# Attention results in other PSUM banks, and four merge gate units inside the NSA loop

## The chip, the cores and the metric
One core of one Trainium2 chip runs the whole program. The metric is the device time of one execution in microseconds (us); of the kernel before it was taken three times, and the median is used. TensorE is called PE, VectorE DVE, ScalarE ACT, GpSimd POOL and SyncE SP, as in the profile.

## The reference, cut to what matters
Three layers over 512 tokens of width 1024, float32: an HGRN2 layer with a SwiGLU feed-forward, a dilated-window attention layer with another, and a layer that adds two mixers, NSA (block-sparse attention) and GLA, through learned merge gates. The two parts that the change touches:

```python
# layer 2: 12 heads, in 3 groups of 4 with windows of dilation 1, 4 and 16
q, k = apply_rope(u @ w_q), apply_rope(u @ w_k); v = u @ w_v
for group, heads in enumerate(...):            # softmax over its own window
    out_g, lse_g = dilated_window_group(q, k, v, window, dilation)
alpha = softmax(lse, over the three groups)    # weighs the groups
h = h + (o * alpha) @ w_out
# layer 3: merge of the two mixers
gate_a, gate_b = split(sigmoid(u @ w_merge))   # each 1024 wide
merged = gate_a * (o_nsa @ w_up_nsa) + gate_b * (o_gla @ w_up_gla)
x = x + merged @ w_out
```

## The kernel before, in words
Activations lie feature-major, [128 partitions, chunk, 512 tokens]. To keep float32 accuracy each projection is made of three products per chunk of 128 features: high weight by high activation, high by low, low by high. `unit(section, k, act, bank)` is one output tile of 128 features: 8 chunks of 3 products, into one PSUM bank (there are 8, `ps[:, bank]`); lines 412 to 414.

**Weights.** SP streams each unit's weights into a ring of 4 slots, each load behind `w_used` (units that PE has finished). ACT casts them to the high half (`hi`, L1102), POOL subtracts to get the low half (`lo`, L1583). There are two slots for split weights, so the cast of unit n+2 waits until PE has used unit n, and PE waits on `w_lo`. `ahead(section, k)` is that cast or subtraction for the unit two after k. The queues of ACT and POOL are in program order, so the place of each `hi` and `lo` in them matters.

**Attention.** V is made token-major, group by group, in four banks each: 0 to 3, 4 to 7, 0 to 3 (L626 to L628); ACT evicts them (L1329, semaphore `av_ready`, 4 for each group). Then 24 `qk_tile`s follow, six for each head step j. Tile N goes to bank N % 4; ACT copies it (`take_raw`, L1341), DVE multiplies by the sine (L2094), POOL by the cosine (L1684), DVE adds (L2101, `qk_ready`). Tile 0 waits until all of V is evicted, tiles from 4 on until DVE has read the bank's last tenant (`rope_sin`).
A head step j on PE is: three QK tiles of step j+1, `attn_scores(j)` (L675 to L683, into banks 4 to 7: group 0 in 4 and 5, group 1 in 6, group 2 in 7), three more QK tiles (in step 3 four tiles of the output projection), and `attn_core(j)`. There PE transposes the probabilities back into the same banks (L706), for groups 1, 2 and 0; ACT copies each to SBUF (L1374, L1374, L1372 for the two banks of group 0; `pt_ready`), and PE multiplies by V (L715 for groups 1 and 2, L718 and L721 for group 0) into bank 4 + g. All values wait for all three copies, since group 1's bank 5 and group 2's bank 6 still hold transposes of others. ACT takes the results (L1379, `ao_hi`), DVE the rest (`ao_rest`, L2154, `ao_lo`), and `attn_out` (L696 to L698) multiplies them with w_out: units 0 to 3 and 8 to 11 take heads 0 and 1, units 4 to 7 and 12 to 15 heads 2 and 3. Unit 4 waits for all twelve results.
On DVE a step is: two ropes, `masked_max` for three groups, a rope, `mix_tops`, `weigh`, two ropes, `ao_rest`, a rope.

**NSA loop.** 24 steps, six for each of four pairs of heads, (query tile, branches) in the order 3a, 3b, 0ab, 2a, 2b, 1ab. In step e PE makes `nsa_scores(e + 2)` (L1005), `nsa_transposes(e)` (L1017), `nsa_values(e - 1)` (L1033) and `gate_chunks(e)`. DVE scales the probabilities (`nsa_scale`, L2425), ahead of each step's transposes, masks and reduces the scores, and adds a pair's values once per pair (`nsa_add`, L2435); ACT takes exponentials (L1521) and copies transposes (L1529). `gate_chunks` puts 1 to 3 chunks of a merge gate unit (a `unit("merge", k)`, 8 chunks, bank 7) behind the values of a step, as `GATE_AT` says: {step: (unit, first chunk, last + 1)}. When a unit is complete, DVE reads it (`merge_raw`, L2441), and the next unit waits for that.
**Merge loop.** For each of 8 output tiles j: gate units (j, 0) and (j, 1) unless made in the NSA loop, then one up-projection unit (L1083 to L1085), sigmoids on ACT (L1561), products and sum on DVE (L2469, L2470, L2475). The host lays out the merge weights in the order of use, which `merge_at(j, k)` mirrors.

Of the kernel before, what the change touches and what calls it, by code (L numbers as in the profile page):

```python
# [4 lines left out]
F32 = mybir.dt.float32  # L5
# [6 lines left out]
P = 128  # L12
# [81 lines left out]
def program(nc, a, out):  # L94
# [20 lines left out]
    with ExitStack() as ctx:  # L115
# [45 lines left out]
        def views(used=0):  # L161
            at = [used]

            def take(*shape):
# [8 lines left out]
                if len(shape) == 3:  # L173
# [79 lines left out]
        prob = shared[:, 0:3072].rearrange("p (a h n) -> p a h n", a=3, h=2)  # L253
        probT = shared[:, 3072:5120].rearrange("p (a h n) -> p a h n", a=2, h=2)

        GATES = ((0, 0), (0, 1), (1, 0))
        GATE_AT = {0: (0, 0, 3), 1: (0, 3, 4), 2: (0, 4, 6), 3: (0, 6, 7), 4: (0, 7, 8),
                   7: (1, 0, 1), 8: (1, 1, 3), 9: (1, 3, 4), 10: (1, 4, 5), 11: (1, 5, 7), 12: (1, 7, 8),
                   15: (2, 0, 1), 16: (2, 1, 2), 17: (2, 2, 4), 18: (2, 4, 5), 19: (2, 5, 6), 20: (2, 6, 8)}
        GATE_END = {4: 0, 12: 1, 20: 2}  # L260

        def merge_at(j, k):

            return {(1, 0): 2, (0, 2): 3}.get((j, k), 3 * j + k)

        TILE_STEPS = ((3, (0,)), (3, (1,)), (0, (0, 1)), (2, (0,)), (2, (1,)), (1, (0, 1)))
        PER_PAIR = len(TILE_STEPS)
# [23 lines left out]
        take = views(used=2 * HC * T)  # L291
        msig, mtmp = take(4, T), take(2, T)
        assert 2 * HC * T + 6 * T <= 28 * T

        def tokens(g, b):

# [95 lines left out]
        def _(pe):  # L392
# [265 lines left out]
                    used(m)  # L658

            def qk_tile(N):  # L660
                if N >= 4:
                    pe.wait_ge(s["rope_sin"], 2 * (N - 3))
                elif N == 0:
                    pe.wait_ge(s["av_ready"], GROUPS * TT)
                used(unit("attn_qk", N, us, N % 4))

            def attn_scores(j):
                pe.wait_ge(s["qk_ready"], 6 * (j + 1))
# [18 lines left out]
            def attn_out(k):  # L687

                n, second = k // 8 * 4 + k % 4, k % 8 // 4
                rr, v, _ = split_use("attn_out", k)  # L690
                pe.wait_ge(s["w_lo"], v)
                rows = ps[:, n].rearrange("p (b m) -> p b m", b=TT)
                for c in range(6):
                    g, j, w = c % 3, 2 * second + c // 3, slice(c * P, (c + 1) * P)
                    oh, ol = ao_split[:, 0, g * HPG + j], ao_low(g, j)
                    nc.tensor.matmul(ps[:, n], ws[:, 0, rr, w], oh, start=not second and c == 0, stop=False)  # L696
                    nc.tensor.matmul(rows, ws[:, 0, rr, w], ol, start=False, stop=False)
                    m = nc.tensor.matmul(ps[:, n], ws[:, 1, rr, w], oh, start=False, stop=second == 1 and c == 5)  # L698
                used(m)

            def attn_core(j):
                for n, g in enumerate((1, 2, 0)):
                    pe.wait_ge(s["p_norm"], 2 * j + 1 + (g == 0))
                    for b in range(TT):
                        for half in range(2 if g == 0 else 1):
                            m = nc.tensor.transpose(SC_BANKS[g][:, b, half * P:(half + 1) * P],  # L706
                                                    SC[g][:, b, half * P:(half + 1) * P], ident[:])
                    m.then_inc(s["pt_ps"], 1)
                for n, g in enumerate((1, 2, 0)):
                    hd = slice(j * P, (j + 1) * P)  # L710
                    pe.wait_ge(s["pt_ready"], 3 * j + (n + 1 if g == 0 else 3))
                    for b in range(TT):
                        o = ps[:, 4 + g, b * P:(b + 1) * P]
                        if g:
                            m = nc.tensor.matmul(o, aV[:, g, b, hd], PTs[:, (g + 1) * T + b * P:(g + 1) * T + (b + 1) * P],  # L715
                                                 start=True, stop=True)
                        else:
                            m = nc.tensor.matmul(o, aV[:, 0, b, hd], PTs[:, b * 2 * P + P:(b + 1) * 2 * P],  # L718
                                                 start=True, stop=b == 0)
                            if b:  # L720
                                m = nc.tensor.matmul(o, aV[:, 0, b - 1, hd], PTs[:, b * 2 * P:b * 2 * P + P],  # L721
                                                     start=False, stop=True)
                    m.then_inc(s["ao_ps"], 1)
# [3 lines left out]
            for j in range(HPG):  # L727
                N = 6 * (j + 1)
                if j + 1 < HPG:
                    for n in range(3):  # L730
                        qk_tile(N + n)
                attn_scores(j)
                if j + 1 < HPG:
                    for n in range(3, 6):
                        qk_tile(N + n)
                else:
                    pe.wait_ge(s["ao_lo"], GROUPS * 2)
                    for k in range(4):
                        attn_out(k)
                attn_core(j)  # L740
            pe.wait_ge(s["ao_lo"], GROUPS * HPG)
            for k in range(4, 2 * DC):
                attn_out(k)
            ffn(1, 4, 3)
# [348 lines left out]
        def _(act):  # L1093
# [241 lines left out]
            def take_raw(N, weights=True):  # L1335
                if weights:
                    qk_weights(N + 2)
                act.wait_ge(s["w_used"], FIRST["attn_qk"] + N + 1)
                if N >= 2:
                    act.wait_ge(s["qk_ready"], N - 1)  # L1340
                nc.scalar.copy(raw[:, N % 2], ps[:, N % 4]).then_inc(s["raw_ready"], 1)  # L1341

            def exps(j, g):
                act.wait_ge(s["sc_negmax"], 3 * j + g + 1)
# [7 lines left out]
            for j in range(HPG):  # L1352
                N, more = 6 * (j + 1), j + 1 < HPG
                if more:
                    for n in range(3):
                        take_raw(N + n)
                exps(j, 0)
                exps(j, 1)
                act.wait_ge(s["mix_diff"], j + 1)
                nc.scalar.activation(e_mix, e_mix, ACT.Exp).then_inc(s["mix_exp"], 1)  # L1360
                qk_weights(N + 5) if more else hi("attn_out", 2)
                exps(j, 2)
                if more:
                    take_raw(N + 3, weights=False)
                    take_raw(N + 4)
                else:
                    for k in range(3, 6):
                        hi("attn_out", k)
                for n, g in enumerate((1, 2, 0)):
                    act.wait_ge(s["pt_ps"], 3 * j + n + 1)  # L1370
                    if g == 0:
                        nc.scalar.copy(PTs[:, 0:1024], ps[:, 4:6].rearrange("p a n -> p (a n)")).then_inc(s["pt_ready"], 1)  # L1372
                    else:
                        nc.scalar.copy(PTs[:, (g + 1) * T:(g + 2) * T], ps[:, 5 + g]).then_inc(s["pt_ready"], 1)  # L1374
                if more:
                    take_raw(N + 5)
                for n, g in enumerate((1, 2, 0)):
                    act.wait_ge(s["ao_ps"], 3 * j + n + 1)
                    nc.scalar.copy(in_order(ao_split[:, 0, g * HPG + j]), by_query(g, ps[:, 4 + g])).then_inc(s["ao_hi"], 1)  # L1379
            act.wait_ge(s["qk_ready"], 24)  # L1380
            act.wait_ge(s["sc_masked"], GROUPS * HPG)
            for dst, name in ((rot_n, "rot_n"), (cos_n, "cos_n"), (sin_n, "sin_n"), (cmp_mask, "cmp_mask"),
# [169 lines left out]
                    outputs_hi(HEADS_G + (e - 15) // 2)  # L1552
            outputs_hi(HEADS_G + 2)
            outputs_hi(HEADS_G + 3)

            for j in range(DC):
                for k in range(2):
# [18 lines left out]
        def _(pool):  # L1576
# [168 lines left out]
            for n in range(2 * HEADS_G):  # L1745
                if n == HEADS_G:
                    ahead("merge", 0)
                if n == HEADS_G + 2:
                    ahead("merge", 1)
                pool.wait_ge(s["up_hi"], n + 1)  # L1750
                f = n if n < HEADS_G else UP_ORDER[n - HEADS_G]
                low, up, src = (go_lo, go_hi, goT) if n < HEADS_G else (oa_lo, oa_hi, oaT)
                nc.gpsimd.tensor_tensor(low[:, f], src[:, f], up[:, f].bitcast(F32), ALU.subtract).then_inc(s["up_lo"], 1)
            for j in range(DC):
                for n in {0: (2, 3), 1: (4, 5)}.get(j, range(3 * j, 3 * j + 3)):
                    ahead("merge", n)
                pool.wait_ge(s["m_hi"], j + 1)
                nc.gpsimd.tensor_tensor(hid[:, 1, j], mtmp[:, j % 2], hid[:, 0, j].bitcast(F32), ALU.subtract  # L1758
# [6 lines left out]
        def _(dve):  # L1765
# [324 lines left out]
            def rope(N):  # L2090
                dve.wait_ge(s["raw_ready"], N + 1)
                for lower in (0, 64):
                    src, dst = slice(lower, lower + 64), slice(64 - lower, 128 - lower)
                    nc.vector.tensor_tensor(tsin[dst, N % 2], ps[src, N % 4], sin_a[src], ALU.mult  # L2094
                                            ).then_inc(s["rope_sin"], 1)
                dve.wait_ge(s["rope_sin"], 2 * N + 2)
                dve.wait_ge(s["rope_cos"], N + 1)
# [52 lines left out]
            def ao_rest(j):  # L2150
                for n, g in enumerate((1, 2, 0)):
                    dve.wait_ge(s["ao_hi"], 3 * j + n + 1)
                    low = ao_low(g, j).rearrange("p b (m r) -> p b m r", r=RESIDUES)
                    nc.vector.tensor_tensor(low, by_query(g, ps[:, 4 + g]), in_order(ao_split[:, 0, g * HPG + j].bitcast(F32)),  # L2154
                                            ALU.subtract).then_inc(s["ao_lo"], 1)

            for n in range(6):
# [448 lines left out]
```

## Time and profile before

| | |
|---|---|
| median of three executions | 2213.12 us (2212.46 to 2219.25) |
| the profiled execution | 2218.95 us, its span 2217.1 us |
| mean granted clock of TensorE | 0.99 of full speed |
| busy: PE, DVE, ACT, POOL | 97%, 47%, 38%, 53% of the span |
| memory traffic | 87 GB/s over the span |

Where the stages lie in the span: V up to 767, QK tiles and head steps from 771 to 975, the output projection behind them, NSA loop from 1590 to 1682, merge loop to 1804. A row of a timeline shows the start of a group of instructions, its length, and in brackets the idle time of its engine just before it with what ended that. Products of PE overlap: a 128x512 product is shown as 0.39 us long, but the next one starts sooner, so the pace is read from starts. [...]

### The profile page before, as it was taken

How to read it: one execution, taken by the hardware profiler on the slowest of the kernel's cores; microseconds unless marked ns; L12 is line 12 of the kernel's file. 1: busy time of each engine (PE TensorE's matmuls, PEld its weight loads, DVE VectorE, ACT ScalarE, POOL GpSimd, SP SyncE). 2: the span in 40 equal slices, each digit the busy share in tenths (PEclk: the TensorE clock that was granted, in tenths of full speed). 3: DMA queues.
4: the chain of work that ended last, by engine and by line, in shares of the span. 5: the costliest groups of instructions: out<-in, count | busy, mean ns of one | idle time of the engine just before them, and what ended most of it. 6: DMA issues, size and time to landing. Idle time of an engine off the chain costs nothing. (4 is left out here: it accounts for less than half of the span.)

```text
span 2217.1 us, 28302 instructions
## 1 busy us (share of the span) xinstructions
PE 2157.2 (97%) x10458; PEld 1779.5 (80%) x10458; DVE 1050.2 (47%) x1483; ACT 852.3 (38%) x1209; POOL 1173.3 (53%) x635
## 2 busy tenths in 40 slices
PE   8999999999999999999999999989999999999997
PEld 6788878888888988778888888778767888888886
DVE  7766774422433047754431446464684344422433
ACT  6565644322233234434321233344664334222222
POOL 5868755554554355535554555473214555554552
PEclk9999999999999999999999999999999999999999
DMA  4112213332332222123332332323101223332331
GB/s 166 58 57 66 65 59 95 95 111 88 95 111 80 86 86 76 58 73 103 95 113 84 97 109 81 126 60 96 67 20 62 100 90 91 102 102 89 95 111 69
DMA packets 52822, 193.30 MB, mean 87 GB/s; under 512 B 6768, under 2 KB 7680, under 8 KB 52480
## 3 DMA queue, kind: packets, MB, share of 16 engines
q1 hardware_dynamic: 50688, 184.95, 26.8%
q10 hardware_dynamic: 2048, 7.19, 0.8%
q8 instruction: 56, 0.92, 0.2%
q14 instruction: 30, 0.25, 0.0%
HBM read 187.92 MB, written 4.19 MB: 87 GB/s over the span
## 5 line engine op out<-in xcount | busy, mean ns | idle before, releaser
L1583 POOL TENSOR_TENSOR w_split<-ring,w_split 128x1024 fp32r<-128x1024 f32 (+3 forms) x327 | 842.8, 2578 | 825.9 <-ACT w_split L1102 825.8
L1102 ACT CAST w_split<-ring 128x1024 fp32r<-128x1024 f32 (+3 forms) x327 | 356.3, 1090 | 1009.0 <-PE ps L414 870.7
L412 PE MATMUL ps<-u_split,w_split 128*128 128x512 f32 x1768 | 707.4, 400 | 15.6 <-DVE u_split L1795 10.7
L414 PE MATMUL ps<-u_split,w_split 128*128 128x512 f32 x1768 | 692.5, 392 | 0.0
L413 PE MATMUL ps<-u_split,w_split 128*128 128x512 f32 x1768 | 692.2, 392 | 0.0
L412 PEld LDWEIGHTS ps<-u_split,w_split 128*128 128x128 f32 x1768 | 334.6, 189 | 93.2 <-issue 18.7
L414 PEld LDWEIGHTS ps<-u_split,w_split 128*128 128x128 f32 x1768 | 334.2, 189 | 71.3
L413 PEld LDWEIGHTS ps<-u_split,w_split 128*128 128x128 f32 x1768 | 334.9, 189 | 69.8 <-issue 3.1
L412 PE MATMUL ps<-hid,w_split 128*128 128x512 f32 x648 | 254.0, 392 | 4.3 <-DVE arena L2080 2.8
L414 PE MATMUL ps<-hid,w_split 128*128 128x512 f32 x648 | 252.7, 390 | 0.0
L413 PE MATMUL ps<-hid,w_split 128*128 128x512 f32 x648 | 252.7, 390 | 0.0
L1877 DVE TENSOR_TENSOR arena<-arena 128x512 f32<-128x512 f32 x66 | 161.9, 2454 | 66.1 <-ACT arena L1193 66.1
L1875 DVE TENSOR_TENSOR arena<-ps,rs_norm 128x512 f32<-128x512 f32 x66 | 45.6, 692 | 258.5 <-PE ps L414 236.4
L412 PEld LDWEIGHTS ps<-hid,w_split 128*128 128x128 f32 x648 | 121.9, 188 | 30.5 <-DVE arena L2080 3.2
L414 PEld LDWEIGHTS ps<-hid,w_split 128*128 128x128 f32 x648 | 122.0, 188 | 25.5
L413 PEld LDWEIGHTS ps<-hid,w_split 128*128 128x128 f32 x648 | 122.1, 188 | 25.4 <-issue 0.2
L1856 DVE TENSOR_TENSOR arena<-arena,ps 128x512 f32 x28 | 19.3, 688 | 187.5 <-PE ps L414 187.5
L1610 POOL TENSOR_TENSOR hid<-arena,hid 128x512 f32 (+1 forms) x66 | 85.2, 1292 | 5.8 <-ACT hid L1197 5.8
L1643 POOL TENSOR_TENSOR arena<-arena 128x256 f32<-128x256 f32 x70 | 62.9, 898 | 46.1 <-ACT arena L1217 46.1
L1881 DVE TENSOR_TENSOR arena<-ps,rs_norm 128x512 f32<-128x512 f32 x66 | 45.6, 691 | 81.6 <-PE ps L414 81.6
L2094 DVE TENSOR_TENSOR arena<-ps,mixer_consts 64x512 f32<-64x512 f32 x48 | 33.0, 688 | 88.0 <-ACT arena L1341 86.9
L1217 ACT ACTIVATE arena<-arena 128x1024 f32<-128x1024 f32 (+2 forms) x40 | 41.9, 1058 | 71.2 <-DVE arena L1922 68.0
(312 smaller groups left out, 2608.4 us busy)
## 6 DMA issues: line engine op xcount, KB each, us to landing
ring<-in_w_hgrn SPq DMA_DIRECT2D x32, 512.0 KB, 3.5
ring<-in_w_attn_qk SPq DMA_DIRECT2D x24, 512.0 KB, 3.6
ring<-in_w_merge SPq DMA_DIRECT2D x24, 512.0 KB, 3.2
ring<-in_w_gu0a SPq DMA_DIRECT2D x22, 512.0 KB, 3.5
ring<-in_w_gu0b SPq DMA_DIRECT2D x22, 512.0 KB, 3.5
ring<-in_w_gu1a SPq DMA_DIRECT2D x22, 512.0 KB, 3.6
ring<-in_w_gu1b SPq DMA_DIRECT2D x22, 512.0 KB, 3.5
ring<-in_w_gu2a SPq DMA_DIRECT2D x22, 512.0 KB, 3.6
```

The source lines that it names most:

```text
L412: nc.tensor.matmul(ps[:, bank], ws[:, 0, r, w], act[:, 0, c], start=c == 0, stop=False)
L413: nc.tensor.matmul(ps[:, bank], ws[:, 0, r, w], act[:, 1, c], start=False, stop=False)
L414: m = nc.tensor.matmul(ps[:, bank], ws[:, 1, r, w], act[:, 0, c], start=False, stop=c == n - 1)
L1102: nc.scalar.copy(ws[:, 0, slot, 0:w], ring[:, r, 0:w]).then_inc(s["w_hi"], 1)
L1217: nc.scalar.activation(dv[:, lo:hi], dv[:, lo:hi], ACT.Exp).then_inc(s["dec_out"], 1)
L1583: nc.gpsimd.tensor_tensor(ws[:, 1, slot, 0:w], ring[:, r, 0:w], ws[:, 0, slot, 0:w].bitcast(F32), ALU.subtract).then_inc(s["w_lo"], 1)
L1610: nc.gpsimd.tensor_tensor(dst, gtmp[:, j % 2], src.bitcast(F32), ALU.subtract).then_inc(s["g_lo"], 1)
L1643: nc.gpsimd.tensor_tensor(x[:, :, 0], x[:, :, 0], kk[:, :, 0], ALU.mult)
L1875: nc.vector.tensor_tensor(gnorm[:, x], ps[:, 2 * x], rs[:], ALU.mult).then_inc(s["gate_norm"], 1)
L1877: nc.vector.tensor_tensor(sgate[:, x], sgate[:, x], gnorm[:, x], ALU.mult).then_inc(s["gate_silu"], 1)
L1881: nc.vector.tensor_tensor(gtmp[:, x], ps[:, 2 * x + 1], rs[:], ALU.mult).then_inc(s["up_norm"], 1)
L2094: nc.vector.tensor_tensor(tsin[dst, N % 2], ps[src, N % 4], sin_a[src], ALU.mult).then_inc(s["rope_sin"], 1)
```

## The change
Nothing is computed differently; it moves results to other banks, waits to other places and one gate unit from the merge loop to the NSA loop.
- QK tiles 0 to 3 go to banks 4 to 7, tiles 4 to 7 to banks 0 to 3 (`qk_bank`). Tile 0 waits for two groups of V, tile 4 for the third; the wait for the rope begins at tile 8.
- Values of groups 0, 1 and 2 go to banks 4, 6 and 7 (`AO_BANK`), and each group waits for its own transposes.
- `attn_out` waits for the results head by head, ahead of each three chunks.
- A fourth gate unit, (1, 1), runs in the NSA loop. Each of four pairs of heads holds one unit, in pieces of 1, 1, 3, 1 and 2 chunks in its first five steps, and none in the sixth. The order of the merge weights, ACT's casts and POOL's subtractions follow.

```diff
-        GATES = ((0, 0), (0, 1), (1, 0))
-        GATE_AT = {0: (0, 0, 3), 1: (0, 3, 4), 2: (0, 4, 6), 3: (0, 6, 7), 4: (0, 7, 8),
-                   7: (1, 0, 1), 8: (1, 1, 3), 9: (1, 3, 4), 10: (1, 4, 5), 11: (1, 5, 7), 12: (1, 7, 8),
-                   15: (2, 0, 1), 16: (2, 1, 2), 17: (2, 2, 4), 18: (2, 4, 5), 19: (2, 5, 6), 20: (2, 6, 8)}
-        GATE_END = {4: 0, 12: 1, 20: 2}
+        GATES = ((0, 0), (0, 1), (1, 0), (1, 1))
+        GATE_AT = {0: (0, 0, 3), 1: (0, 3, 4), 2: (0, 4, 6), 3: (0, 6, 7), 4: (0, 7, 8)}
+        for k in range(1, 4):
+            for n, (lo, hi) in enumerate(((0, 1), (1, 2), (2, 5), (5, 6), (6, 8))):
+                GATE_AT[6 * k + n] = (k, lo, hi)
+        GATE_END = {6 * k + 4: k for k in range(4)}
         def merge_at(j, k):
-            return {(1, 0): 2, (0, 2): 3}.get((j, k), 3 * j + k)
+            return 2 * j + k if j < 2 and k < 2 else 4 + j if j < 2 else 3 * j + k
...
+        AO_BANK = (4, 6, 7)
+        def qk_bank(N):
+            return 4 + N if N < 4 else N % 4
...
             def qk_tile(N):
-                if N >= 4:
+                if N >= 8:
                     pe.wait_ge(s["rope_sin"], 2 * (N - 3))
-                elif N == 0:
-                    pe.wait_ge(s["av_ready"], GROUPS * TT)
-                used(unit("attn_qk", N, us, N % 4))
+                elif N % 4 == 0:
+                    pe.wait_ge(s["av_ready"], (3 if N else 2) * TT)
+                used(unit("attn_qk", N, us, qk_bank(N)))
...
                     g, j, w = c % 3, 2 * second + c // 3, slice(c * P, (c + 1) * P)
+                    if c % 3 == 0:
+                        pe.wait_ge(s["ao_lo"], GROUPS * (j + 1))
...
-                    pe.wait_ge(s["pt_ready"], 3 * j + (n + 1 if g == 0 else 3))
+                    pe.wait_ge(s["pt_ready"], 3 * j + n + 1)
                     for b in range(TT):
-                        o = ps[:, 4 + g, b * P:(b + 1) * P]
+                        o = ps[:, AO_BANK[g], b * P:(b + 1) * P]
...
-                    pe.wait_ge(s["ao_lo"], GROUPS * 2)
                     for k in range(4):
                         attn_out(k)
                 attn_core(j)
-            pe.wait_ge(s["ao_lo"], GROUPS * HPG)
             for k in range(4, 2 * DC):
                 attn_out(k)
...
             outputs_hi(HEADS_G + 2)
             outputs_hi(HEADS_G + 3)
+            ahead("merge", 3)
...
             for n in range(2 * HEADS_G):
                 if n == HEADS_G:
                     ahead("merge", 0)
+                    ahead("merge", 1)
                 if n == HEADS_G + 2:
-                    ahead("merge", 1)
+                    ahead("merge", 2)
...
             for j in range(DC):
-                for n in {0: (2, 3), 1: (4, 5)}.get(j, range(3 * j, 3 * j + 3)):
+                for n in {0: (3, 4), 1: (5,)}.get(j, range(3 * j, 3 * j + 3)):
                     ahead("merge", n)
```
ACT's copies and DVE's reads use `qk_bank` and `AO_BANK` in the same way, and the host's list of merge weights becomes `[0, 1, 3, 4, 2, *range(5, 24)]`.

## Rows read from the trace of the kernel before

**Rows 1.** The page: busy time, share of the span and instructions by engine.
```profile
PE 2157.2 (97%) x10458; PEld 1779.5 (80%) x10458; DVE 1050.2 (47%) x1483; ACT 852.3 (38%) x1209; POOL 1173.3 (53%) x635
```
**Rows 2.** PE's waits: waiting line, releaser, us in total, times, longest.
```profile
PE ps L715 <- ACT arena L1372: 4.4, 4, 1.1
PE ps L683 <- DVE arena L2101: 3.6, 1, 3.6
```
**Rows 3.** Timeline of PE from V to QK: start, length, group, idle before.
```profile
767.44 0.40 PE L628 MATMUL ps<-w_split,u_split 128*128 128x512 f32 x1
771.29 0.80 PE L412 MATMUL ps<-u_split,w_split 128*128 128x512 f32 x1 [3.46 <-ACT arena L1329]
...
774.98 0.39 PE L412 MATMUL ps<-u_split,w_split 128*128 128x512 f32 x1
```
**Rows 4.** Timeline of PE in the merge loop: first product of two units.
```profile
1688.79 0.47 PE L412 MATMUL ps<-u_split,w_split 128*128 128x512 f32 x1 [0.83 <-POOL w_split L1583]
...
1694.32 0.39 PE L1083 MATMUL ps<-go_hi,w_split 128*128 128x512 f32 x1
```
**Rows 5.** Windows: length, busy PE, PEld, DVE, ACT, POOL, granted clock, DMA, GB/s.
```profile
772.00:777.00 5.00, 5.00 (x18) 4.01 (x17) 0.00 (x0) 0.00 (x0) 0.00 (x0) 0.74 0.00 0
...
1613.00:1621.00 8.00, 5.39 (x52) 3.67 (x52) 7.32 (x13) 6.24 (x18) 2.61 (x2) 1.00 0.02 7
1675.00:1683.00 8.00, 5.85 (x65) 4.41 (x62) 4.77 (x11) 5.33 (x12) 0.00 (x0) 1.00 0.10 40
...
1620.69:1624.99 4.30, 4.30 (x24) 2.57 (x24) 2.02 (x6) 2.65 (x6) 1.46 (x2) 0.60 0.01 2
```
**Rows 6.** Timelines of ACT and POOL behind the last V product.
```profile
767.87 1.04 ACT L1102 CAST w_split<-ring 128x1024 fp32r<-128x1024 f32 x1 [4.59 <-PE ps L628]
...
768.99 2.35 POOL L1583 TENSOR_TENSOR w_split<-ring,w_split 128x1024 fp32r<-128x1024 f32 x1 [3.24 <-ACT w_split L1102]
```
**Rows 7.** Timeline of PE in attention: values, scores, output projection.
```profile
937.07 2.05 PE L715 MATMUL ps<-arena 128*128 128x128 f32 x16 [1.10 <-ACT arena L1372]
...
944.33 0.71 PE L683 MATMUL ps<-arena 128*128 128x128 f32 x4 [3.64 <-DVE arena L2101]
...
975.18 0.50 PE L696 MATMUL ps<-ao_split,w_split 128*128 128x512 f32 x1 [1.40 <-DVE ao_split L2154]
```
**Rows 8.** Timelines of ACT and DVE in head steps 2 and 3.
```profile
936.01 1.01 ACT L1372 COPY arena<-ps 128x1024 f32<-128x1024 f32 x1 [0.24 <-PE ps L706]
...
938.45 1.74 DVE L2101 TENSOR_TENSOR arena<-arena 128x512 f32<-128x512 f32 x1
940.22 1.89 DVE L2154 TENSOR_TENSOR ao_split<-ps,ao_split 128x512 fp32r<-128x512 f32 x3
...
943.58 0.69 DVE L2101 TENSOR_TENSOR arena<-arena 128x512 f32<-128x512 f32 x1
...
974.43 0.69 DVE L2154 TENSOR_TENSOR ao_split<-ps,ao_split 128x512 fp32r<-128x512 f32 x1 [0.87 <-ACT ao_split L1379]
```
**Rows 9.** Timeline of PE in the NSA loop, steps 1, 5 to 7, 22.
```profile
1598.21 0.50 PE L412 MATMUL ps<-u_split,w_split 128*128 128x512 f32 x1
...
1599.11 0.92 PE L1005 MATMUL ps<-arena 64*128 64x384 f32 x4
...
1613.36 0.72 PE L1005 MATMUL ps<-arena 64*128 64x128 f32 x8 [0.29 <-ACT arena L1529]
1614.28 1.11 PE L1017 MATMUL ps<-ident_sb,arena 128*128 128x128 f32 x8 [0.20 <-DVE arena L2425]
...
1618.69 0.66 PE L1017 MATMUL ps<-ident_sb,arena 128*128 128x128 f32 x4 [1.28 <-DVE arena L2425]
1620.11 0.66 PE L1017 MATMUL ps<-ident_sb,arena 128*128 128x128 f32 x4 [0.75 <-DVE arena L2425]
...
1677.25 0.94 PE L1017 MATMUL ps<-ident_sb,arena 128*128 128x128 f32 x6 [1.86 <-DVE arena L2425]
```
**Rows 10.** Timeline of DVE ahead of that last row.
```profile
1675.92 0.68 DVE L2441 TENSOR_TENSOR arena<-ps,rs_norm 128x512 f32<-128x512 f32 x1
```

More of the change, by code:

```diff
@@ L1340, in take_raw @@
                     act.wait_ge(s["qk_ready"], N - 1)
-                nc.scalar.copy(raw[:, N % 2], ps[:, N % 4]).then_inc(s["raw_ready"], 1)
+                nc.scalar.copy(raw[:, N % 2], ps[:, qk_bank(N)]).then_inc(s["raw_ready"], 1)
             def exps(j, g):
@@ L1378, in _ @@
                     act.wait_ge(s["ao_ps"], 3 * j + n + 1)
-                    nc.scalar.copy(in_order(ao_split[:, 0, g * HPG + j]), by_query(g, ps[:, 4 + g])).then_inc(s["ao_hi"], 1)
+                    nc.scalar.copy(in_order(ao_split[:, 0, g * HPG + j]), by_query(g, ps[:, AO_BANK[g]])).then_inc(s["ao_hi"], 1)
             act.wait_ge(s["qk_ready"], 24)
@@ L2093, in rope @@
                     src, dst = slice(lower, lower + 64), slice(64 - lower, 128 - lower)
-                    nc.vector.tensor_tensor(tsin[dst, N % 2], ps[src, N % 4], sin_a[src], ALU.mult
+                    nc.vector.tensor_tensor(tsin[dst, N % 2], ps[src, qk_bank(N)], sin_a[src], ALU.mult
                                             ).then_inc(s["rope_sin"], 1)
@@ L2153, in ao_rest @@
                     low = ao_low(g, j).rearrange("p b (m r) -> p b m r", r=RESIDUES)
-                    nc.vector.tensor_tensor(low, by_query(g, ps[:, 4 + g]), in_order(ao_split[:, 0, g * HPG + j].bitcast(F32)),
+                    nc.vector.tensor_tensor(low, by_query(g, ps[:, AO_BANK[g]]), in_order(ao_split[:, 0, g * HPG + j].bitcast(F32)),
                                             ALU.subtract).then_inc(s["ao_lo"], 1)
@@ L2559 @@
     arrays["w_merge"] = np.ascontiguousarray(
-        np.stack([fm(wmerge[:, :D]), fm(wmerge[:, D:]), fm(up)], 1).reshape(3 * DC, P, D)[[0, 1, 3, 2, *range(4, 3 * DC)]])
+        np.stack([fm(wmerge[:, :D]), fm(wmerge[:, D:]), fm(up)], 1).reshape(3 * DC, P, D)[[0, 1, 3, 4, 2, *range(5, 3 * DC)]])
     arrays["w_mix_out"] = fm(g["w_out_2"][0])
```

## The prediction, made before the result was known
> **What bounds the kernel now.** I read the page first. The reader is to see that TensorE (PE) is busy for 2157.2 us of a span of 2217.1 [rows 1]: the time is TensorE's work plus some 60 us of holes. The change neither adds nor removes a matrix product; it can only close or open holes, change the clock in them, and move work into or out of them. PE's waits give the names: values of attention behind ACT's copies (L715), scores behind DVE's rope (L683) [rows 2]. Then I took the timeline of PE stage by stage, and those of ACT, DVE and POOL beside each hole, to see which chain ends it. A hole closes only if that chain gets shorter, or if other PE work is put into it.
>
> **Part 1, the border from V to QK.** The last V product starts at 767.44, the first QK product at 771.29, after 3.46 idle that ACT's evictions (L1329) end. The nine starts after it take 3.69 us [rows 3], where products at full pace come 0.23 apart, 2.07 for nine [rows 4]. [...] Now QK tile 0 goes to bank 4, whose tenants (V group 1) were evicted a group earlier, and waits for those alone. Following directly, its tenth product would start at 767.44 + 10 x 0.23 + 0.1 for the change of section = 769.8 instead of 774.98: 5.2 us. What else could hold it? Its own weights: POOL stood idle for 3.24 us before 768.99, so residue 0 was done at 765.8. For tile 1, ACT casts from 767.87 and POOL subtracts until 771.3 [rows 6]; tile 0 takes 24 x 0.23 = 5.5 us, to 773.2, so they are in time. The four evictions of group 2 run beside tile 0, and tile 4 is the first that needs their banks. The rope wait dropped at tiles 4 to 7 is worth nothing: no hole stands there. Gain 5.2; 3.6 if only the hole came back and not the clock.
>
> **Part 2, values after their own transposes.** In each of the four head steps PE stands 1.10 us before L715 because all three copies must be in; the last (L1372) runs 936.01 to 937.02 [rows 7, 8]. With group 1 in bank 6 and group 2 in bank 7, these two start when the transposes end, at 937.07 - 1.10 = 935.97; their copies stand ahead of L1372 on ACT and are in. Their 16 products take some 1.9 us, more than the 1.0 that ACT still needs for group 0. So the 1.10 is filled, four times. Where does it go? After head steps 0 and 1 three QK tiles (16 us) run before the next scores, no hole stands there, and the 1.10 stays. After step 2 it does not: the scores of step 3 wait 3.64 us for DVE's last rope. DVE has no gap ahead of it: L2101 from 938.45, L2154 three times in 1.89 us from 940.22, and the last rope until 944.27 [rows 8]. It comes to L2154 late by its own chain, so earlier values only make the hole 4.74. Gain 0 there, and the clock falls as before. In step 3 the 1.10 counts. Sum 3 x 1.10 = 3.3; bounds 2.2 (step 3 lost too) and 4.4 (step 2 kept).
>
> **Part 3, attn_out by its own heads.** Tile 4 of the projection waits 1.40 us for the last L2154 [rows 7]. Its first three chunks now need head 2 only, and last 9 x 0.23 = 2.1 us. The last L2154 ran 974.43 to 975.12 [rows 8] and comes 1.1 earlier with the values, so it ends inside those 2.1 us. Gain 1.4, bounds 0 and 1.4. ACT's casts and SP's loads behind w_used move with it. Attention in all: 5.2 + 3.3 + 1.4 = **9.9**.
>
> **Part 4, the gate unit.** A unit lasts from 1688.79 to 1694.32, 5.5 us [rows 4], in a merge loop with no hole behind it, so taking one out gives 5.5. What does the NSA loop grow by? A lone chunk between two steps takes 0.90 (1598.21 to 1599.11 [rows 9]), one in company 3 x 0.23 = 0.68. The eight chunks more, by place:
> - Step 6 gets one, ahead of the transposes of step 7, which stand 1.28 and 0.75 for DVE's scaling [rows 9]. DVE's chain there begins with the values of step 5, ahead of the chunk. Hidden: 0.
> - Step 21 gets one, ahead of the hole of 1.86. DVE runs a gate read (L2441, 0.68) just before that scaling, and the read moves to step 23 [rows 9, 10]. The hole shrinks by 0.6 and hides the chunk: minus 0.6.
> - The other six (net of what leaves steps 11 and 17) stand where there is no hole: 6 x 0.68 = 4.1, and 0.25 for three more pieces (20, before 17), between 0 and 3 x 0.22.
> - Steps 11 and 17 have no chunk now. Step 5 shows what such a step is like: 0.29 behind ACT's copy and 0.2 behind DVE [rows 9]. Twice: 1.0, bounds 0 and 2 x 0.75, the larger hole of step 7.
> - Three chunks in one step hand DVE its next scores 0.7 later. DVE's waits for scores there are longer than 1 us: nothing.
> - The clock was 0.60 from 1620.69 to 1624.99, so low for 0.8 of 4.3 us [rows 5]. Work at half pace for 3.4 us loses 1.7 at most, and I take 1.5, since the gaps between products are not all clocked. PE was busy 5.39 of the 8 us to 1621; with the chunk it is 6.15, and a stretch with 5.85 kept the clock [rows 5]. I take it as kept.
>
> Growth 4.1 + 0.25 + 1.0 - 0.6 - 1.5 = 3.3, gain 5.5 - 3.3 = **2.2**; with the fall, 0.7.
>
> Moved along: ACT's cast and POOL's residue of the merge weights, from steps 14 and 22 to 12 and 18, and one behind the loop. There ACT's cast (1.04 [rows 6]) now stands before its two sigmoids, which DVE reads for the first merge; TensorE asks for that merge only two units later, so nothing. POOL's last residue keeps its place, so the 0.83 at 1688.79 stays [rows 4]. SP's loads wait for w_used as before and only change order.
>
> POOL's residue beside DVE's scaling needs a word: POOL holds 2.35 for one [rows 6], and L2101 took 1.74 at 938.45 beside POOL where 0.69 is usual [rows 8]. A collision can thus cost 0 to 2.4. The two moved residues meet the scaling of steps 14 and 20, which have a chunk ahead of them now; I take 0, and 2.4 for the range. [...]
>
> **Sum.** 9.9 + 2.2 = 12.1. The profiled execution took 2218.95, 5.8 over the median of 2213.12; the same holes are taken to stand in both. 2213.1 - 12.1 = **2201.0**.
>
> **Rivals.**
> - A: as above, clock kept or lost at step 7: 2201.0 to 2202.5. Chance 0.55.
> - B: the NSA loop is paced by DVE and ACT more than by PE. For it: DVE busy 7.32 of 8 us in one stretch [rows 5]. Then the clock fall (1.5), a collision (2.4) and longer chunk-less steps (0.5) are paid, part 4 ends at -2.2 to 0, and the time is 2203 to 2205.5. Against it: DVE busy only 4.77 in the other [rows 5]. Chance 0.20.
> - C: the border stays open, because something else stands 3 us late there (tile 1's cast, or a load). Then 4.7 + 2.2 remain: 2206.2. With it the case that nothing arrives, to 2213. Rows 6 speak against it. Chance 0.11.
> - D: step 2 keeps its 1.10, and the low clock after that hole goes as well: 2198 to 2200. Against it: DVE's unbroken chain. Chance 0.11.
> - E, on the other side: the clock. [...] By 1.5 in 4.3 us, each low microsecond costs 0.35. It eats up 12.1 from 35 low microseconds on, over a third of the loop of some 90; the whole loop would give 2201 + 31 = 2232. Chance 0.03: the loop shows one fall of 4.3 us [rows 5]. [...]
>
> **Range.** What can be told from no change is 0.3%, 6.6 us, so faster means below 2206.5. A, B and D lie there (0.86): faster 0.86, same 0.11, slower 0.03. The range takes in A, B, D and the better edge of C: 2197 to 2208.
>
> **What would show it.** No L412 behind L1329, and a clock of 1.0 after the V stage; no L715 behind L1372; L683 behind L2101 about 4.7; no L696 behind L2154; in the NSA loop small holes after steps 5, 11 and 17, and one under 0.6 before step 22's transposes; the merge loop 5.5 shorter. The forecast is wrong if a new wait stands before QK tile 1, if head steps 0 or 1 hand their 1.10 back before the next scores, or if DVE's scaling is stretched by 2 us.

## The result and the profile after

The changed kernel takes 2199.81 us (median of 4, 2198.46 to 2200.06) against 2212.79 for the kernel before beside it (median of 4, 2211.91 to 2219.25): a ratio of 0.9929, 95% interval 0.9909 to 0.9949, 13.0 us less. The forecast was 2201.0, range 2197 to 2208. The profiled execution of the changed kernel took 2200.06, with a span of 2198.2. Its span is 18.9 shorter than that of before; 6.4 of those lie in a stage that the change does not touch, and differ nearly as much (6.2) between two executions of the changed kernel, as a later section shows.

The page's busy line of the changed kernel, against [rows 1], shows the same 10458 products and 7.4 us less of busy TensorE:
```profile
PE 2149.8 (98%) x10458; PEld 1774.3 (81%) x10458; DVE 1050.7 (48%) x1483; ACT 851.5 (39%) x1209; POOL 1174.7 (53%) x635
```
PE's busy time falls although its work is the same, because more of it ran at a low granted clock before, where a 128x512 product is shown as 0.63 long instead of 0.39. Most of that lies in the GLA stage (granted clock 0.93 against 0.96 over some 150 us), not in the stages of the change. Of PE's waits, against [rows 2] (waiting line, releaser, us in total, times, longest), the one of the values on ACT's copies is gone, and the one of the scores on DVE has grown:
```profile
PE ps L690 <- DVE arena L2110: 5.0, 1, 5.0
PE ps L1024 <- DVE arena L2434: 3.5, 9, 0.8
```
The changed kernel has other line numbers. Scores are L690 there (L683 before), transposes of attention L715 (L706), values L724 (L715), the output projection L705 (L696), the rope's addition L2110 (L2101); in the NSA loop scores are L1012 (L1005), transposes L1024 (L1017), and DVE's scaling L2434 (L2425).

**The border.** Timeline of PE, where [rows 3] had a hole of 3.46:
```profile
767.46 0.39 PE L635 MATMUL ps<-w_split,u_split 128*128 128x512 f32 x1
767.69 0.40 PE L419 MATMUL ps<-u_split,w_split 128*128 128x512 f32 x1
```
The first QK product starts 0.23 after the last V product, as far behind it as that one behind its own neighbour (767.23 to 767.46). The window behind it (length, busy PE, PEld, DVE, ACT, POOL, granted clock, DMA, GB/s), against the first of [rows 5]:
```profile
772.00:777.00 5.00, 5.00 (x24) 4.13 (x23) 1.38 (x2) 1.53 (x2) 2.53 (x2) 1.00 0.35 105
```
The granted clock, a share of full speed, is 1.00 where it was 0.74. In the profile of before the window from 771.3 to 774.3 has 0.50, and its products start 0.43 apart; from 775 to 778 it has 1.00, and they start 0.23 apart.

**Attention.** Timeline of PE: the scores of head step 3, then the transposes, values and output projection of step 3, against [rows 7]:
```profile
936.38 1.22 PE L690 MATMUL ps<-arena 128*128 128x128 f32 x4 [5.01 <-DVE arena L2110]
...
960.05 1.91 PE L715 MATMUL ps<-ident_sb,arena 128*128 128x128 f32 x16
961.80 1.95 PE L724 MATMUL ps<-arena 128*128 128x128 f32 x16
...
964.92 0.39 PE L730 MATMUL ps<-arena 128*128 128x128 f32 x2
965.07 0.48 PE L705 MATMUL ps<-ao_split,w_split 128*128 128x512 f32 x1
```
The values stand without a wait behind the transposes, tile 4 of the projection without a wait behind the values. The hole ahead of the last scores is 5.01 long.

**The NSA loop.** Timeline of PE around steps 5 to 7, and ahead of the transposes of step 22, against [rows 9]:
```profile
1596.81 0.72 PE L1012 MATMUL ps<-arena 64*128 64x128 f32 x8 [0.30 <-ACT arena L1536]
1597.73 1.12 PE L1024 MATMUL ps<-ident_sb,arena 128*128 128x128 f32 x8 [0.21 <-DVE arena L2434]
...
1602.16 0.66 PE L1024 MATMUL ps<-ident_sb,arena 128*128 128x128 f32 x4 [0.55 <-DVE arena L2434]
1603.57 0.66 PE L1024 MATMUL ps<-ident_sb,arena 128*128 128x128 f32 x4 [0.75 <-DVE arena L2434]
...
1662.31 0.94 PE L1024 MATMUL ps<-ident_sb,arena 128*128 128x128 f32 x6 [0.36 <-DVE arena L2434]
```
The first two rows are a step with no chunk ahead of it; much the same pair of holes (0.30, 0.21) comes back at 1621.70 and 1645.48, behind steps 11 and 17. The 1.28 of before is 0.55, the 1.86 is 0.36. The granted clock, mean of 88 us of the loop from its start, was 0.98 before and is 1.00:
```profile
1573.00:1661.00 88.00, 82.37 (x636) 54.05 (x632) 72.25 (x139) 56.70 (x151) 18.12 (x11) 1.00 0.11 40
```

**Where the time went.** Distances between starts of the same product in each profile, in us. The scores are taken at their 128x256 products, 0.44 behind their first one, in both profiles. The GLA stage is the stretch ahead of the NSA loop, in which the recurrence of GLA runs; it is taken from the first 128x280 product (the NSA token projection) to the first gate product. NSA goes from there to the first product of the first up-projection unit, merge from there to the product of the section behind it that waits 1.39 for POOL's `hid`.

| stage | before | after | difference |
|---|---|---|---|
| last V product to the scores of step 0 | 54.92 | 49.65 | -5.27 |
| head steps 0 and 1 | 90.34 | 87.63 | -2.71 |
| scores of step 2 to first projection tile | 37.91 | 38.77 | +0.86 |
| first projection tile to tile 4 | 24.58 | 21.56 | -3.02 |
| tile 4 to the GLA stage | 465.01 | 464.94 | -0.07 |
| GLA stage | 150.35 | 143.96 | -6.39 |
| NSA loop | 91.68 | 94.66 | +2.98 |
| merge loop | 121.77 | 116.39 | -5.38 |

The four rows of attention give 10.1, the gate part 2.4. The GLA stage, which the change doesn't touch, gives 6.4 in this pair of executions.

### The profile page after: what moved, and what is told of

It is laid out like the page before. It is cut to its first block and busy times, and to the rows that moved or that the text cites. A ratio compares the mean times of both kernels' runs of the same rounds, so it can differ in the third digit from the quotient of the medians.

```text
span 2198.2 us, 28314 instructions
## 1 busy us (share of the span) xinstructions
PE 2149.8 (98%) x10458; PEld 1774.3 (81%) x10458; DVE 1050.7 (48%) x1483; ACT 851.5 (39%) x1209; POOL 1174.7 (53%) x635
```

## The experiments

The theory was that of the prediction: each of the four parts closes its own holes, and the parts add up. The rivals were that the gain has one main source (the clock behind the border), that parts only shift each other's holes, and, once the traces stood side by side, that the GLA stage is changed by it. Ratios are against the kernel before on the same chip, which took 2218.2 to 2218.4 in the median there.

**Each part alone** (before, with one part of the change):
```
p1_qk      used(unit("attn_qk", N, us, qk_bank(N)))     # and its two waits, ACT's copy, DVE's read
p2_values  pe.wait_ge(s["pt_ready"], 3 * j + n + 1)     # and AO_BANK in its four places
p3_proj    if c % 3 == 0: pe.wait_ge(s["ao_lo"], GROUPS * (j + 1))   # in place of the two waits
p4_gate    the gate table, merge_at and ahead of the diff, attention as before
```

> The kernel before with the banks of the first eight QK tiles alone. Theory of the prediction: 5.2 us less than before (hole 3.6 and low clock 1.6), scores of head step 0 start 5.2 earlier, granted clock 1.0 right behind V. Rival C: the hole comes back before tile 1 and under 2 us are gained. Rival 'hole without clock': 3.6. Beside it, a second theory on the 5.8 us by which the profiled execution of before lies over the median: a vector addition at L1921 took 8.87 us there while GpSimd worked without a pause; if that is what makes two sorts of executions, a profile with that instruction under 3 us has a wait of under 3 us at the pair scores behind it and belongs to a time near the median, whatever the kernel.

> The kernel before with the value banks and their own waits alone. Theory of the prediction: 3.3 us less (head steps 0, 1 and 3 keep 1.1 each, step 2 gives it back: the wait of the scores of step 3 grows from 3.6 to 4.7). The wait for the last output results before the projection stays at 1.4. Rival D: 4.4 less, that wait stays 3.6. Rival that all is given back: no change.

> The kernel before with the waits of the output projection head by head alone. Theory of the prediction: 1.4 us less, no wait at its fifth unit. Rival: the wait moves to the fourth chunk of that unit and less than 0.5 is gained.

> The kernel before with the fourth gate unit in the NSA loop alone. Theory of the prediction: 2.2 us less, with holes of 0.3 and 0.2 in steps 6, 12 and 18, under 0.6 before the transposes of step 22, and full clock at 1620. With the low clock kept, 0.7 less. Rival B: 0 to 2 us more, scaling on VectorE stretched by 2 us beside GpSimd's moved residues. [...]

| kernel | median us | ratio, 95% interval | stages in its profile |
|---|---|---|---|
| p1_qk | 2214.47 (12) | 0.9985, 0.9976 to 0.9993 | V to scores 49.64 |
| p2_values | 2214.45 (12) | 0.9980, 0.9971 to 0.9991 | steps 0 and 1 87.61, projection 23.21 |
| p3_proj | 2217.22 (11) | 0.9994, 0.9985 to 1.0003 | projection 22.92 |
| p4_gate | 2215.49 (12) | 0.9985, 0.9977 to 0.9994 | NSA 94.63, merge 116.37 |
| before | 2218.43 (35) | | |

The medians lose 4.0, 4.0, 1.2 and 2.9, together 12.1; the four parts are about additive, and no part has most of it. (One of the 12 executions of p2_values took 5555.84; without it the median is 2214.36, and its ratio leaves it out.) Alone, p3_proj can't be told from no change by its time, only by its stage, which loses 1.66. The stage of p1_qk loses 5.2 to 5.3 against the four profiles with 54.87 to 54.97, and 6.5 to 6.6 against those of p2_values and p4_gate, where the same hole of 3.46 is followed by a longer low clock and the stage lasts 56.11 and 56.27. p1_qk's median loses only 4.0; its interval, 1.6 to 5.3, just reaches the loss of the stage, and why the whole gains less than the stage stays open. Its profile can't settle this, because the profiled execution took 2203.71, 10.8 less than the kernel's own median. Against the profile of before it also has a GLA stage of 142.32 (8.0 less), an NSA loop that keeps its clock (1.5 less) and 0.9 more behind step 2. The expectation on record, that a profile with a short L1921 belongs to a time near the median, was a miss.

In p2_values the last scores wait as long as in the changed kernel. Timeline of its PE:
```profile
941.58 1.23 PE L685 MATMUL ps<-arena 128*128 128x128 f32 x4 [5.00 <-DVE arena L2103]
```
So it is the earlier values alone that lengthen this hole, as the prediction had it for step 2.

**The old gate pieces keep or lose the clock.** The windows of 88 us over the NSA loop, of p2_values, p1_qk and p4_gate:
```profile
1586.00:1674.00 88.00, 80.85 (x618) 52.99 (x620) 71.63 (x144) 57.96 (x159) 14.88 (x10) 0.98 0.11 39
```
```profile
1576.00:1664.00 88.00, 80.62 (x637) 52.79 (x634) 74.01 (x147) 58.96 (x160) 15.38 (x10) 1.00 0.11 39
```
```profile
1590.00:1678.00 88.00, 82.40 (x629) 54.21 (x628) 72.28 (x139) 57.00 (x151) 17.66 (x11) 1.00 0.10 39
```
With the pieces of before, the clock fell in three profiles (before, p2_values, p3_proj: loops of 91.68, 93.09, 93.17), once in the first and twice in the other two, and stayed in two (p1_qk and the kernel called handover below: 90.17 and 90.15). The first fall comes behind the holes of 1.28 and 0.75 at step 7. The second comes behind the hole of 1.86 ahead of the transposes of step 22, near the end of the windows above or behind it. Of p2_values, the hole and the window behind it:
```profile
1672.90 1.01 PE L1019 MATMUL ps<-ident_sb,arena 128*128 128x128 f32 x6 [1.86 <-DVE arena L2427]
```
```profile
1673.00:1677.00 4.00, 4.00 (x26) 3.24 (x26) 1.80 (x6) 2.37 (x6) 0.00 (x0) 0.58 0.02 4
```
With the new pieces, which shorten both holes, it stayed at 1.00 in six profiles (after, p4_gate and the four kernels after_again, after_hand, fill and fill_hand below), and their loops last 94.58 to 94.66. So the loop grows by 4.5 against one that keeps its clock. NSA and merge loop together last 211.96 in p1_qk and 211.00 in p4_gate, so part 4 is worth 1.0 there; it is worth 2.4 against the profile of before, and 3.9 against p2_values and p3_proj. The 2.9 of p4_gate's median lies among them.

**One chunk moved in the loop of before.** Which edit removes the fall? The hole of 1.28 at step 7 stands ahead of the first one, so this kernel only puts the old unit 1's first chunk into step 6:
```
-                   7: (1, 0, 1), 8: (1, 1, 3), ...
+                   6: (1, 0, 1), 8: (1, 1, 3), ...
```

> The kernel before with one chunk of the second gate unit moved from step 7 to step 6, ahead of the hole of 1.28 before the transposes of step 7. Theory: the chunk is hidden in the hole, 0.55 is left of it, 0.7 to 0.8 us less; and the clock, which fell right behind this hole in three of the five profiles with the old pieces and in none of five with the new ones, stays, so that the loop takes 89.4 (90.2 without a fall before, 91.7 to 93.2 with one). Rival: the fall has nothing to do with this hole and comes as before.

Timeline of its PE, against the fifth and sixth of [rows 9]:
```profile
1616.76 0.66 PE L1017 MATMUL ps<-ident_sb,arena 128*128 128x128 f32 x4 [0.55 <-DVE arena L2425]
1618.18 0.66 PE L1017 MATMUL ps<-ident_sb,arena 128*128 128x128 f32 x4 [0.76 <-DVE arena L2425]
```
Its clock is 1.00 over the loop, which lasts 89.61: 0.55 less than the two old loops that kept theirs, and 2.1 less than that of before. The median loses 1.9 (2216.26 against 2218.18, ratio 0.9990, 0.9981 to 0.9999). The first fall of the three profiles comes behind this hole of 1.28, so that shortening it removes that fall is likely, but not shown: the old loop keeps its clock in two profiles of five with the hole in place, and this is one profile. The hole ahead of step 22 is still 1.85 in it, and the clock did not fall there.

**The changed kernel once more, and the GLA stage.** The kernel after_again is the changed kernel, unedited.

> The changed kernel once more, beside the others. The four parts measured alone gave, start to start in their own stages, 5.3 to 6.6 (border), 1.4 in each of three head steps (values), 1.7 (projection with its own waits) and 1.0 plus a low clock of 1.5 to 3 (gate unit): 12 to 17 us less than before on the same chip. A second theory on the spread of the executions: VectorE's addition L1930, the first of the second head pair's level exponents, is 2.5 us long in some executions and 8.9 in others; where it is 8.9, the stage from the NSA token projection to the NSA loop is 149 to 150 us, else 142 to 144.

It took 2205.04 (5 runs) against 2218.28, ratio 0.9941, 0.9928 to 0.9955: 13.2 less, much as in the first measurement (13.0), but 5.2 more than it took there. Its attention, NSA and merge stages agree within 0.06 with those of the first profile. The GLA stage lasts 150.15 instead of 143.96. In it one addition on DVE differs. Timelines of DVE and POOL in the profile of before:
```profile
1460.79 8.87 DVE L1921 TENSOR_TENSOR arena<-arena 128x256 f32<-128x256 f32 x1
```
```profile
1460.56 2.39 POOL L1583 TENSOR_TENSOR w_split<-ring,w_split 128x1024 fp32r<-128x1024 f32 x1
1462.91 0.84 POOL L1643 TENSOR_TENSOR arena<-arena 128x256 f32<-128x256 f32 x1
1463.71 0.85 POOL L1644 TENSOR_TENSOR arena<-arena 128x256 f32<-128x256 f32 x1
1464.51 2.56 POOL L1637 TENSOR_TENSOR arena<-arena 128x512 f32<-128x512 f32 x2
1466.99 2.38 POOL L1583 TENSOR_TENSOR w_split<-ring,w_split 128x1024 fp32r<-128x1024 f32 x1
```
The addition starts 0.23 after POOL's residue (its subtraction for the low half of weights) and ends at 1469.66, 0.29 after POOL first pauses (1469.37). Its next neighbours take 0.41. In the profile of after the same addition, 0.22 behind the same residue, ends at 1453.07, 0.28 after that one instruction (to 1452.79):
```profile
1450.60 2.47 DVE L1930 TENSOR_TENSOR arena<-arena 128x256 f32<-128x256 f32 x1
```
PE's pair scores behind it wait 4.93 in before and 0.94 and then 1.37 in after. That is 2.6 of the 6.4. The rest, 3.8, goes with TensorE's clock, which was lower for longer behind the longer wait. Windows of 10 us around the pair scores, before and after:
```profile
1472.00:1482.00 10.00, 9.22 (x52) 7.78 (x54) 7.17 (x20) 1.41 (x2) 2.96 (x4) 0.54 0.01 2
```
```profile
1464.00:1474.00 10.00, 9.08 (x51) 7.33 (x53) 8.32 (x16) 3.24 (x4) 5.75 (x5) 0.83 0.16 52
```
Over the whole stage the granted clock is 0.93 and 0.96.

**A wait that keeps POOL away.** If POOL's unbroken work is the cause, then POOL, told to stand still for DVE's four additions, gives the short outcome every time. The kernel handover is the kernel before with one wait on GpSimd, behind the residue:
```
+            def hand_over():
+                ahead("nsa_tm", 1)
+                pool.wait_ge(s["dec_in"], 8 * (HEADS_H + 1) + 2)
```
after_hand is the changed kernel with the same wait.

In numbers, what was expected of handover: the addition under 2.5 us in every execution, PE's wait behind it down from 4.9 to under 1.5, all times 4 to 7 us under the median of before; if POOL has no part in it, no change, or 1.4 us more.

> The kernel before, with one wait more on GpSimd: behind one weight residue, amid a run of nine multiplications, it waits until VectorE has written two levels of the second head pair. [...]

> The changed kernel with the same wait on GpSimd. Theory: the same gain where the changed kernel's executions are in the upper group, 1 to 2 us where they are in the lower one; the spread of its times is under 3 us. Rival: no change.

Timelines of DVE and POOL in handover:
```profile
1460.16 2.44 DVE L1925 TENSOR_TENSOR arena<-arena 128x256 f32<-128x256 f32 x1
1462.53 0.41 DVE L1926 TENSOR_TENSOR arena<-arena 128x256 f32<-128x256 f32 x1
```
```profile
1463.69 0.84 POOL L1643 TENSOR_TENSOR arena<-arena 128x256 f32<-128x256 f32 x1 [1.36 <-DVE arena L1926]
```
POOL's residue runs from 1459.94 to 1462.33, and the addition ends 0.27 after it. POOL gives up 1.36 and PE's wait is 1.67. The GLA stage lasts 141.61 and 141.69. The medians lose 6.5 (2211.83 against 2218.28, ratio 0.9970, 0.9958 to 0.9981) and 6.8 (2198.24 against 2205.04 of after_again). The gain is much the same with and without the change, so the GLA stage is its own matter. The addition is not all that varies: the 7 times of handover still spread over 6.2 us (2207.56 to 2213.73, 4.6 to 10.7 under the median of before, where 4 to 7 was expected), and the 4 of after_hand over 3.4, where under 3 was expected.

**The hole ahead of the last scores.** It is what is left of attention's waits, 5.01, and it is DVE's. The kernel fill puts PE work into it: the first tile of the output projection, which needs heads 0 and 1 only, runs ahead of the scores of step 3 instead of behind them; ACT's casts move along.
```
+                else:
+                    pe.wait_ge(s["rope_sin"], 2 * 21)
+                    attn_out(0)
                 attn_scores(j)
...
-                    for k in range(4):
+                    for k in range(1, 4):
                         attn_out(k)
```
fill_hand has the wait on GpSimd as well.

> The changed kernel with the first unit of the output projection moved ahead of the scores of head step 3, into the 5.0 us hole behind VectorE's rope, and ACT's casts for units 2 and 3 earlier. Theory: head step 2's gain did come, and was stored as a wait. The unit's 4.1 us fill the hole, 0.6 to 1 is left of it, the clock does not fall behind it (0.9 us of 6.1 from those scores to the projection), and up to 1.2 us come back as a wait of the group 0 transposes of step 3, now 4 us earlier: 3.5 to 5 us less than the changed kernel. Rival: VectorE's chain from the scores of step 3 is the bound, and all but the clock comes back as a wait at the transposes: under 1.5 us less.

> Both additions to the changed kernel at once: the projection unit ahead of the scores of head step 3, and GpSimd's wait. Theory: they touch different stages and add up, 5.4 and 6.8 less than the changed kernel's upper group: 2191.5 to 2194 where the kernel before takes 2218, and no execution over 2196. Rival: a part of the fill is given back later; over 2196.

Timeline of PE in fill, and the window behind it:
```profile
933.61 0.39 PE L707 MATMUL ps<-ao_split,w_split 128*128 128x512 f32 x1
934.88 0.71 PE L690 MATMUL ps<-arena 128*128 128x128 f32 x4 [0.89 <-DVE arena L2118]
```
```profile
936.00:942.00 6.00, 6.00 (x28) 5.67 (x27) 4.97 (x7) 2.56 (x11) 0.75 (x1) 1.00 0.11 42
```
In the changed kernel the window behind the hole has a granted clock of 0.50:
```profile
936.00:941.00 5.00, 4.62 (x15) 4.08 (x16) 1.13 (x2) 0.00 (x0) 0.00 (x0) 0.50 0.00 0
```
The tile takes 4.1 us of the hole, the low clock goes with it, and no new wait stands before the transposes of step 3, where up to 1.2 was expected to come back; from the last V product to the GLA stage fill needs 656.70 instead of 662.53, 5.8 less. The medians: fill 2199.65 (ratio 0.9916, 0.9903 to 0.9930), 5.4 less than after_again, a little over the 3.5 to 5 expected; fill_hand 2192.03 (0.9880, 0.9865 to 0.9895), 13.0 less, on another chip. The two edits about add up (5.4 and 6.8 make 12.2).

**Other pieces.** best_21 is fill_hand with the eight chunks of gate units 1 to 3 in another order, so that two instead of one stand in the first step:
```
-            for n, (lo, hi) in enumerate(((0, 1), (1, 2), (2, 5), (5, 6), (6, 8))):
+            for n, (lo, hi) in enumerate(((0, 2), (2, 3), (3, 5), (5, 6), (6, 8))):
```

> The same, with the gate pieces of head pairs 1 to 3 in 2, 1, 2, 1, 2 chunks in place of 1, 1, 3, 1, 2: one chunk moves from the third step of each pair to its first, ahead of the holes of 0.55, 0.43 and 0.54 before the transposes of the second step. Theory (those holes are ended by VectorE's scaling, whose chain starts ahead of the chunk): the three holes are filled, 1.3 to 1.7 us less from the start of the NSA loop to the merge's end (204.6 before). Rival (the chain is PE's own, or the third step then starves): no gain, or a wait in the third step.

Timeline of its PE at step 7:
```profile
1594.81 0.66 PE L1027 MATMUL ps<-ident_sb,arena 128*128 128x128 f32 x4
1596.15 0.65 PE L1027 MATMUL ps<-ident_sb,arena 128*128 128x128 f32 x4 [0.68 <-DVE arena L2446]
```
The 0.55 is gone, and so are the 0.43 and 0.54 that fill_hand shows at 1618.77 and 1642.68; its second hole at step 7, 0.76 in fill_hand, is 0.68. The loop lasts 92.77 instead of 94.63, 1.9 less, a little over the 1.3 to 1.7 expected. The median is 2190.82 (4 runs, 2189.99 to 2191.83) against 2192.03; the ratio 0.9875 (0.9860 to 0.9890) overlaps with fill_hand's 0.9880, and only the stage tells the two apart. It is the fastest kernel of the study: 27.4 less than the kernel before beside it, 14.2 less than after_again, which ran on another chip.

## Why the prediction was right, point by point

- **Part 1, 5.2 forecast.** It measured 5.27 in the pair of profiles. Of the two bounds, the one with the clock was right: the hole and the low clock (0.50 from 771.3 to 774.3 before, 1.00 from 770 to 780 now) went together. Tile 1 did not wait, and nothing else stood late there; rival C did not come. What the rows of before could not tell is that the low clock behind this hole lasts longer in some executions, so the part is worth 5.3, or 6.5 to 6.6. Its kernel alone gained less, 4.0, as said above.
- **Part 2, 3 x 1.10 = 3.3 forecast.** The count was right: steps 0, 1 and 3 keep it, step 2 hands it to the scores, whose hole grew from 3.64 to 5.01. That speaks against rival D. The size was too small: 1.37 each, 4.1 in all. The 1.10 is an idle time, reckoned from the modelled end of the last product. From start to start, transposes to values were 967.15 to 970.16 before, 3.01, and are 1.75 now, and the values to the next group went from 1.89 to 1.78 (972.05 - 970.16 and 963.58 - 961.80): 1.37. The same holds for the scores' hole, forecast as 4.74. This is the term that was mis-sized: 3.3 forecast, 4.1 measured.
- **Part 3, 1.4 forecast.** It measured 1.66 in p3_proj, for the same reason. The wait was hidden entirely.
- **Behind step 2.** The stretch from the scores of step 2 to the projection is 0.86 longer in this pair, with a longer low clock behind the lengthened hole: over the 8 us from the start of the scores of step 3 the granted clock is 0.79 before and 0.70 in the changed kernel. But p1_qk and p4_gate, which keep the 3.64, also show the longer stage (38.8) and a granted clock of 0.65 and 0.64 there, so it comes without the change too. Of the six profiles with the 3.64, four have the shorter stage and two the longer; the four with the lengthened hole (p2_values, after, after_again, after_hand) all have the longer one. Whether a longer hole makes it more frequent is not shown.
- **Part 4, 2.2 forecast.** It measured 2.4 in the pair of profiles. The unit saved 5.4 (5.5 forecast). The loop grew by 4.5 without the clock's term (4.75 forecast: 4.1 + 0.25 + 1.0 - 0.6), and the clock's term was 1.5 in the profile of before (91.68 against 90.17), as forecast; the reason given for 1.5 instead of 1.7, gaps that are not all clocked, no run shows. Steps 6 and 21 hid their chunks, and steps 5, 11 and 17 show the pair of 0.30 and 0.21. One scaling on DVE was stretched by 1.8 beside a residue of POOL, close to the 2 us that the prediction had named as a sign of being wrong. In the changed kernel:
```profile
1608.57 2.27 DVE L2434 TENSOR_SCALAR arena<-arena 128x384 f32<-128x384 f32 x1
```
```profile
1608.23 2.40 POOL L1591 TENSOR_TENSOR w_split<-ring,w_split 128x1024 fp32r<-128x1024 f32 x1
```
The mean of this form was 0.49 before. No wait of PE stands behind it, so it cost nothing there; it also shows with the old pieces where the clock stayed (two scalings in 2.64 in p1_qk and handover), so it is not one of the two moved residues. That a collision costs up to 2.4 was the author's estimate from the length of a residue; the addition of 8.87 in the GLA stage shows that this is no bound. POOL's residue ahead of the merge stayed where it was (0.82 at 1675.23). Rival B did not come: PE grew by the chunks' length where no hole stood. E came out the other way round: the new pieces keep the clock in every profile. That the clock might fall at the steps without a chunk and stay low was a guess that no run shows: behind their pauses of 0.2 and 0.3 the granted clock is 1.00. Its price was also too low. It divided the 1.5 by the 4.3 us of a window of which, at 0.60, only 3.4 were low, if the low clock is the 0.50 of 771.3 to 774.3, so a low microsecond cost 0.44 and not 0.35.
- **The sum.** By stages 5.3 + 4.1 + 1.7 + 2.4 = 13.5, less the 0.9 of the low clock behind step 2, is 12.6; the median gave 13.0. The 12.1 was 0.9 short, and four closed holes that cost 0.26 to 0.27 more each than their idle time are 1.1; the rest is within what the clock does from one execution to the next.
- **What it took for granted.** That "the same holes stand" in the profiled execution and in the median. It did not hold: the profile of before holds a hole of 4.93 in the GLA stage whose short form is 2.3. It did little harm here, because the change was priced from its own holes and not from the difference of two spans. Whoever had read the gain off the two profiles would have found 18.9. And there was some luck in the time itself: 2201.0 holds for a chip on which before takes 2213. On another, with 2218.3 for before, the same kernel took 2205.04, 13.2 less.

## What to carry to other kernels

Price a change by the stage that it touches, start to start, and compare only that stage in the two traces. A difference of whole spans can hold a third of its size from an unrelated place. A hole costs more than its idle time where the clock falls behind it: closing the one of 3.46 us, with 0.50 behind it, was worth 5.3 in its stage here. One that can't be closed can be filled with a later tile's work, which was worth 5.8. If a hole is ended by a chain with no gap of its own, speeding up what stands before it gains nothing; the freed time appears in the hole (3.64 became 5.01 here), so look there first for what to move in.

## What the runs showed of the hardware

**A long addition on DVE beside unbroken work on POOL.** A 128x256 addition of two SBUF tiles whose next neighbour, with POOL idle, takes 0.41 us took 8.87 in the profile of before, from 0.23 behind the start of a POOL instruction until 0.29 after POOL's first pause, past six POOL instructions. In the thirteen profiles it took 8.87 to 8.94 in seven, 2.47 and 2.49 in the two others without the added wait, and 2.44 to 2.49 in the four with it. In the short form the addition ended 0.28 after a single residue of 2.41 us (after) and 0.27 after one of 2.39 (handover). In the long form five of POOL's instructions came to their end, each with the next one behind it without a gap in the timeline, and the addition ended behind the sixth only. With POOL standing still behind the residue all four profiles show the short form; what passes between the two engines, no run shows. The distance between the two starts is 0.15 to 0.23 in the seven long ones and 0.18 and 0.22 in the two short ones, so it does not decide between them, and what does stays open. That the medians on two chips differ by 5.2 for the changed kernel (and by 5.5 for the one before) fits two mixtures of the two forms, but the unprofiled executions show no stages, and this is not shown.

**A low clock of different length behind the same hole.** Behind 3.46 us of idle the stage lasted 54.9 to 55.0 in four profiles and 56.1 to 56.3 in two; the granted clock from 770 to 780 was 0.83 in p3_proj and 0.70 in p2_values. In the NSA loop of before, with holes equal to 0.01, the clock did not fall at all (p1_qk, handover: 1.00), fell behind step 7 alone (before, 1.5 us) or behind steps 7 and 22 (p2_values and p3_proj, 2.9 to 3.0 us). The kernel's rows ahead of the fall don't tell which it will be.
